# Rows of the split operands moved to the weights' place modulo 256 bytes

## The reference

```
y = swiglu(rmsnorm(h, g1), w_gu, w_down);  h = h + 0.5 * rmsnorm(y, g2)
proj = rmsnorm(h, g3) @ w_in               # q, k, v of three branches, and gates
branches: neighbourhood, sliding-window and differential attention
          (second stack: sliding-window, forgetting attention, a gated linear recurrence)
merged = sum over n of sigmoid(gate_n) * (branch_n @ w_branch[n])
h = h + rmsnorm(merged @ w_out, g4)
...
swiglu(x) = (silu(x @ w_gate) * (x @ w_up)) @ w_down      # inner width 2816
```

## The kernel before

| tile | before |
|---|---|
| `wh`, `wl` | 128 in every slot and every k |
| `uh`, `ul` row k | 192 + 64 k: 192, 0, 64, 128, 192, ... (rows 2112 bytes apart) |
| `obh`, `obl` row k | 32 + 64 k: 32, 96, 160, 224 |
| `mh`, `ml` row k | 160 + 64 k: 160, 224, 32, 96, ... |
| `gx`, `gb` | 96 (rows 2048 bytes apart) |
| `gu` | 128 (rows 2048 bytes apart) |
| `bh`, `bl` | 96 (rows 1024 bytes in use) |

## Time and profile before

### The profile page before, as it was taken

The page is one execution under the profiler, slowest core; times in us unless marked ns, Lnnn a source line. Parts: engine busy times, 40 slices in busy tenths (PEclk is TensorE's granted clock), DMA queues, the critical chain, the costliest instruction groups (busy, mean ns, idle before and its releaser), DMA issues. The chain is left out here.

```text
span 3400.5 us, 51734 instructions
## 1 busy us (share of the span) xinstructions
PE 3351.0 (99%) x20422; PEld 2960.8 (87%) x20422; DVE 2442.6 (72%) x3936; ACT 1690.7 (50%) x3071; POOL 849.2 (25%) x607
## 2 busy tenths in 40 slices
PE   9999999999999999999999999999999999999998
PEld 7999887888889998999887888899988888888998
DVE  7878765756697769777766666697768676649776
ACT  5545453635454445444554544454546374335543
POOL 3433111021063414432111021063400001206431
PEclk9999999999999999999999999999999999999999
DMA  4333433253223332333423263233333222322332
GB/s 137 106 100 113 115 90 86 67 147 93 82 91 104 108 100 78 103 106 112 117 75 93 70 152 96 69 99 102 105 96 96 86 80 69 106 88 93 98 108 81
DMA packets 118049, 332.79 MB, mean 98 GB/s; under 512 B 18984, under 2 KB 21800, under 8 KB 117808
## 3 DMA queue, kind: packets, MB, share of 16 engines
q1 hardware_dynamic: 105200, 306.30, 28.9%
q0 software_dynamic: 12320, 22.66, 3.2%
q10 hardware_dynamic: 288, 0.52, 0.1%
HBM read 306.23 MB, written 4.21 MB: 91 GB/s over the span
## 5 line engine op out<-in xcount | busy, mean ns | idle before, releaser
L1889 DVE TENSOR_TENSOR wl<-raw,wh 128x1024 fp32r<-128x1024 f32 (+2 forms) x633 | 800.7, 1269 | 277.4 <-ACT wh L1311 271.3
L1311 ACT ACTIVATE wh<-raw 128x1024 fp32r<-128x1024 f32 (+2 forms) x637 | 553.9, 875 | 393.8 <-PE PS L790 385.0
L790 PE MATMUL PS<-bh,wh 128*128 128x256 f32 x2520 | 711.1, 282 | 8.6 <-ACT tmp L1311 5.4
L790 PE MATMUL PS<-bh,wl 128*128 128x256 f32 x2520 | 708.0, 281 | 0.0
L790 PE MATMUL PS<-bl,wh 128*128 128x256 f32 x2520 | 707.9, 281 | 0.0
L790 PE MATMUL PS<-uh,wh 128*128 128x512 f32 (+2 forms) x1656 | 615.6, 372 | 12.0 <-DVE ul L1924 7.0
L790 PE MATMUL PS<-uh,wl 128*128 128x512 f32 (+2 forms) x1656 | 605.1, 365 | 0.0
L790 PE MATMUL PS<-ul,wh 128*128 128x512 f32 (+2 forms) x1656 | 603.6, 364 | 0.0
L790 PEld LDWEIGHTS PS<-bh,wh 128*128 128x128 f32 x2520 | 474.7, 188 | 14.8 <-DVE wl L1889 7.2
L790 PEld LDWEIGHTS PS<-bh,wl 128*128 128x128 f32 x2520 | 474.8, 188 | 0.7
L790 PEld LDWEIGHTS PS<-bl,wh 128*128 128x128 f32 x2520 | 474.8, 188 | 0.0
(11 more groups left out here) (268 smaller groups left out, 5766.3 us busy)
## 6 DMA issues: line engine op xcount, KB each, us to landing
raw<-in_gu SPq DMA_DIRECT2D x218, 512.0 KB, 3.2
raw<-in_win SPq DMA_DIRECT2D x139, 512.0 KB, 3.3
raw<-in_dn SPq DMA_DIRECT2D x80, 320.0 KB, 3.0
raw<-in_dn SPq DMA_DIRECT2D x40, 512.0 KB, 3.7
raw<-in_wbr SPq DMA_DIRECT2D x72, 256.0 KB, 2.7
raw<-in_wout SPq DMA_DIRECT2D x24, 512.0 KB, 3.2
raw<-in_dn SPq DMA_DIRECT2D x40, 256.0 KB, 2.7
raw<-in_wv SPq DMA_DIRECT2D x20, 512.0 KB, 3.2
```

Of the source, the lines that this page charges most:

```text
L790: return e.matmul(out, lhs, rhs, start=start, stop=stop, skip_group_check=True)
L1311: return e.activation(out, in_, f, scale=scale, **more)
L1889: tt(wl[:, c % 4, 0:n], src, wh[:, c % 4, 0:n], SUB).then_inc(*S.lo.up(("lo", c)))
```

## The change

Tiles get other addresses; nothing else is changed. `GAP` is 32 bytes, what takes X from its place (96) to the weights' (128). `uh`, `ul`, `mh`, `ml`, `obh` and `obl` become 512 columns wide, so that rows lie 2048 bytes apart and each begins at 128 modulo 256; `gx` (and behind it `b12`, `b21`) moves on by 32 bytes. v = 6 needs 528 columns and keeps the old rows under the names `uh6`, `ul6` (`y_u5` is what stage 5 leaves in their memory). `gu`, `gb`, `bh`, `bl` and the weights stay. `u_of` and `y_of` pick the tile and shift the columns by X0.

```
-        uh = sb("uh", [P, 8, TW], F32R, where["uh"])
-        ul = sb("ul", [P, 8, TW], F32R, where["ul"])
-        y_u = sb("y_u", [P, 8, TW], F32, where["uh"])
+        uh = sb("uh", [P, 8, 512], F32R, where["uh"])
+        ul = sb("ul", [P, 8, 512], F32R, where["ul"])
+        y_u = sb("y_u", [P, 8, 512], F32, where["uh"])
+        uh6 = sb("uh6", [P, 8, TW], F32R, where["uh"])
+        ul6 = sb("ul6", [P, 8, TW], F32R, where["ul"])
+        y_u5 = sb("y_u5", [P, 8, TW], F32, where["uh"])
...
+        GAP = (where["split"] - X) % 256
...
-        gx = sb("gx", [P, 6, 2, 512], F32R, X + 65536)
+        gx = sb("gx", [P, 6, 2, 512], F32R, X + 65536 + GAP)
...
-        mh = sb("mh", [P, 8, TW], F32R, X)
-        ml = sb("ml", [P, 8, TW], F32R, X + 8 * TW * 4)
+        mh = sb("mh", [P, 8, 512], F32R, X + GAP)
+        ml = sb("ml", [P, 8, 512], F32R, X + GAP + 8 * 2048)
...
-        obh = sb("obh", [P, 4, TW], F32R, XG + 10 * TW * 4)
-        obl = sb("obl", [P, 4, TW], F32R, XG + 14 * TW * 4)
+        XO = XG + 10 * TW * 4 + (GAP + 128) % 256
+        obh = sb("obh", [P, 4, 512], F32R, XO)
+        obl = sb("obl", [P, 4, 512], F32R, XO + 4 * 2048)
...
+        def u_of(v, part, k, c0, c1):
+
+            if v == 6:
+                return (uh6, ul6)[part][:, k, c0:c1]
+            return (uh, ul)[part][:, k, c0 - X0:c1 - X0]
...
+        def y_of(v, m, c0=X0, c1=TW):
+
+            return y_u5[:, m, c0:c1] if v == 5 else y_u[:, m, c0 - X0:c1 - X0]
...
-                            xh, xl = uh[:, kk, c0:c0 + cn], ul[:, kk, c0:c0 + cn]
+                            xh, xl = (u_of(v, i, kk, c0, c0 + cn) for i in range(2))
```

More of the change, by code:

```diff
@@ L816, in dense @@
                             E.wait_ge(S.dv, "m", v, kk)
-                            xh, xl = mh[:, kk, c0:c0 + cn], ml[:, kk, c0:c0 + cn]
+                            xh, xl = mh[:, kk, c0 - X0:c0 - X0 + cn], ml[:, kk, c0 - X0:c0 - X0 + cn]
                         else:
                             E.wait_ge(S.dv, "ob", v, job.tag[2], kk)
-                            xh, xl = obh[:, kk, c0:c0 + cn], obl[:, kk, c0:c0 + cn]
+                            xh, xl = obh[:, kk, c0 - X0:c0 - X0 + cn], obl[:, kk, c0 - X0:c0 - X0 + cn]
                         w1, w2 = wh[:, p % 4, P * k:P * k + P], wl[:, p % 4, P * k:P * k + P]
@@ L882, in first_two @@
                         w1, w2 = wh[:, p % 4, P * k:P * k + P], wl[:, p % 4, P * k:P * k + P]
-                        i = three(bank(job.banks[0]), w1, w2, uh[:, k, X0:TW], ul[:, k, X0:TW], k == 0, k == 7)
+                        i = three(bank(job.banks[0]), w1, w2, uh[:, k, :], ul[:, k, :], k == 0, k == 7)
                         if k == 7:
@@ L1054, in group_out @@
                         w1, w2 = wh[:, p % 4, P * k:P * k + P], wl[:, p % 4, P * k:P * k + P]
-                        i = three(bank(job.banks[0]), w1, w2, mh[:, k, X0:TW], ml[:, k, X0:TW], k == 0, k == 7)
+                        i = three(bank(job.banks[0]), w1, w2, mh[:, k, :], ml[:, k, :], k == 0, k == 7)
                         if k == 7:
@@ L1070, in values @@
                             w1, w2 = wh[:, p % 4, 512 * k2:512 * k2 + 512], wl[:, p % 4, 512 * k2:512 * k2 + 512]
-                            u1, u2 = uh[:, kk, tokens(j)], ul[:, kk, tokens(j)]
+                            u1, u2 = (u_of(v, i, kk, tokens(j).start, tokens(j).stop) for i in range(2))
                             mm(bank(vb[j]), u1, w1, kk == 0, False)
@@ L1377, in last @@
                         E.wait_ge(S.dv, "ev", job.tag, c)
-                        square("post", v, m, y_u[:, m, half(c)], 1.0, c)
+                        square("post", v, m, y_of(v, m, half(c).start, half(c).stop), 1.0, c)
                         return
@@ L1381, in last @@
                     square("post", v, m, o, 0.5, c)
-                    act(y_u[:, m, half(c)], o, ACT.Copy).then_inc(*S.aa.up(("y", v, m, c)))
+                    act(y_of(v, m, half(c).start, half(c).stop), o, ACT.Copy).then_inc(*S.aa.up(("y", v, m, c)))
                 ahead(p0)
@@ L1448, in part @@
                         E.wait_ge(S.mm, "job", job.tag, 0)
-                        act(y_u[:, m, X0:TW], bank(job.banks[0]), ACT.Copy).then_inc(*S.aa.up(("part", job.tag)))
+                        act(y_of(v, m), bank(job.banks[0]), ACT.Copy).then_inc(*S.aa.up(("part", job.tag)))
                 silu_plain(0)
@@ L1527, in out @@
                         square("post", v, m, bank(job.banks[0]), 0.5)
-                        act(y_u[:, m, X0:TW], bank(job.banks[0]), ACT.Copy).then_inc(
+                        act(y_of(v, m), bank(job.banks[0]), ACT.Copy).then_inc(
                             *S.aa.up(("y", v, m, 0)))
@@ L1668, in outputs @@
                         E.wait_ge(S.mm, "job", ("br", v, 0, 7), 0)
-                    act(obh[rows, t, X0:TW], bank(b)[rows, :], ACT.Copy).then_inc(*S.an.up(("oh", v, st, x)))
+                    act(obh[rows, t, :], bank(b)[rows, :], ACT.Copy).then_inc(*S.an.up(("oh", v, st, x)))
             def attention(v, st, fill):
@@ L1845, in mixer_2 @@
                     E.wait_ge(S.dv, "gelu", m, 3)
[L1846 removed]
+                    act(obh[:, m, :], lru[:, 4 + m, X0:TW], ACT.Copy).then_inc(*S.aa.up(("lru", m)))
                 tanh(v, 2, 0)
@@ L1994, in add_part @@
                 last = job.kind == "dn" and v == 7
-                y = h[:, m, c0:c0 + cn] if last else y_u[:, m, c0:c0 + cn]
+                y = h[:, m, c0:c0 + cn] if last else y_of(v, m, c0, c0 + cn)
                 i = tt(y, bank(job.banks[c], 0, cn), y, ADD)
@@ L2431, in rest @@
                     E.wait_ge(S.an, "oh", v, st, x)
-                    tt(obl[rows, t, X0:TW], bank(b)[rows], obh[rows, t, X0:TW], SUB).then_inc(
+                    tt(obl[rows, t, :], bank(b)[rows], obh[rows, t, :], SUB).then_inc(
                         *S.dv.up(("ol", v, st, x), *([("ob", v, BRANCH[st], t)] if x % 2 else [])))
@@ L2538, in low_c @@
                     E.wait_ge(S.an, "c_oh", v, x)
-                    tt(obl[:, x, X0:TW], GB[4 + x][:, X0:TW], obh[:, x, X0:TW], SUB).then_inc(*S.dv.up(("ob", v, 2, x)))
+                    tt(obl[:, x, :], GB[4 + x][:, X0:TW], obh[:, x, :], SUB).then_inc(*S.dv.up(("ob", v, 2, x)))
                 diagonal(0)
@@ L2729, in low_lru @@
                     E.wait_ge(S.aa, "lru", m)
-                    tt(obl[:, m, X0:TW], lru[:, 4 + m, X0:TW], obh[:, m, X0:TW], SUB).then_inc(*S.dv.up(("ob", v, 2, m)))
+                    tt(obl[:, m, :], lru[:, 4 + m, X0:TW], obh[:, m, :], SUB).then_inc(*S.dv.up(("ob", v, 2, m)))
                 ahead(reach(JOBS["g", v, 2, 0]))
```

38 lines of the change are left out of this document (20 added, 18 removed).

## The result

The changed kernel takes 3378.13 us (median of four runs, 3375.52 to 3382.65), against 3398.39 us for the kernel before, measured beside it (four runs, 3395.22 to 3400.6). The ratio is 0.9941, 95% interval 0.9927 to 0.9955: faster by 0.6%. The prediction was 3376 us in a range of 3366 to 3390. The profiled execution spans 3377.6 us, 22.9 less than the one before; the sum of the prediction was 22.8. By the medians the gain is 20.3 us, and the interval of the ratio allows 15 to 25, so the near agreement of 22.9 and 22.8 is more than the runs can vouch for.

What follows compares the result with a forecast made beforehand. TensorE was taken as the bound, busy 3351.0 of 3400.5 us. Terms 7.2 + 3.0 + 7.3 + 3.8 + 2.2 + 1.9 - 2.6 gave 22.8 us, hence 3377.7 profiled, 3376 us as median; range 3366 to 3390.

Steps and rivals of the forecast that it cites:

- The step: TensorE's 512-column matmuls: 226.7 ns each in a long run with all operands at one place modulo 256 bytes.
- gx, 7.2 us: FFN matmuls on gx: 1170 of 1650 gain 6.6 ns each, 7.7 us, less 0.5 us for entries.
- The 0.6 us of part 0: 96 gx matmuls opening each of five FFNs: saving waited for again behind them, counted as nothing; otherwise 3.2 us more.
- no free moment: VectorE during part 0 and behind it: full, 6.00 of 6 us in both stretches shown, so TensorE waits for its splits.
- uh in the mixers, 7.3 us: uh, ul in two mixers, 2 x 1032 matmuls: 4.2 us from fills between attention units, 3.1 from the others.
- the price of an entry: Start of each run at the weights' place: about six matmuls to reach the faster step, 20 ns lost.
- a fill of six: Six matmuls between attention units in the mixers: should take about as long as now.
- uh in the FFNs, obh, mh, values: Other 512-column matmuls: 744 on uh, 864 on obh, 432 on mh, 384 values; gains 3.0, 3.8, 2.2, 1.9 us.
- Halves, 2.6 us lost: 1548 matmuls of 256 columns on uh, gx and mh: 1.7 ns dearer each at the weights' place.
- The projections never settle: Rival: uh, obh, mh and values stay at 230 ns; gain 13.3 us, about 3385 us; chance 0.15.
- Slower: Rival: uh and ul mixed at one place settle on 240 ns, costing 36 us, 3430 us; chance 0.05.
- It does nothing: Rival: gu's step comes from something other than its place modulo 256 bytes; 3398.7 us, chance 0.08.

Runs made afterwards that it cites:

- e1: Loop of matmuls alone, computation left out, moving rows at eight places modulo 256: 48 matmuls of 512 columns take 10.88 us at the weights' place, 11.20 at 160.
- e4: The changed kernel with uh, ul, mh, ml, obh, obl 128 bytes further and gx back at 96: 3401.38 us, ratio 1.0006 to the kernel before.
- e2: The kernel before with gx alone moved by 32 bytes: 3393.4 us, ratio 0.9987.
- e3: The changed kernel with gx back at its old place (96): 3384.36 us, ratio 0.9959 to the kernel before.
- e8: Matmuls alone, stretches of 6 to 48 behind small ones, weights' place against place 96: shorter by 8.5 ns (6), 24 (12), 64 (18), 264 (48).
- e9: The changed kernel with the pairs' operands bh, bl (and gb) at the weights' place too: 3382.39 us, ratio 0.9947 to the kernel before.
- e10: Loop of 256-column matmuls alone at three places, six forms of distances, banks and neighbours: at place 64, 96 matmuls take 11.32 us in e1's form.
- e5: The changed kernel with rb and par moved behind X, so bh and bl lie 64 bytes below the weights: 3376.56 us, ratio 0.9928 to the kernel before.
- e7: e5 with VectorE multiplying only the first 128 of 512 columns of each pair's gated product: 3364.94 us, ratio 0.9895 to the kernel before.

## Why the prediction was right, point by point

**The step.** Right. `gx` at 227.1, values at 226.7, `obh` and `mh` in the two mixers at 230.9 and 226.9 ns with their entries, from 233 to 236 before. e1 and e4 show the cause as it was put: the place against the weights, modulo 256 bytes. Why the chip is faster there no run shows. The Trainium skill ("TensorE: Matmul & The Clock Gate", section "Step-by-step: what each phase is for") has two independent read ports, from which the prediction drew the rival that the place could not matter; the runs here do not agree with that: 226.7 against 233.3 ns for the same instructions.

**gx, 7.2 us.** Right in size and in its cover. The matmuls gained 10.25 us, the pairs gave 3.5 back (3.1 of it in the five gaps), 6.8 in sum. The 0.6 us of part 0 that were to be waited for again are waited for again, in all five FFNs, and e2 and e3 tie that to `gx`. That it is VectorE that they wait for, as the prediction says, is not settled: GpSimd's sums and ScalarE's copy of them come in at the very moment at which VectorE is free (975.53 and 975.52), and no run removed the work of either at this place. Nor has VectorE "no free moment": between the two stretches of the earlier trace rows it stands for 0.52 us until ScalarE's `wh` is there.

```profile
968.47 2.30 DVE L1889 TENSOR_TENSOR wl<-raw,wh 128x512 fp32r<-128x512 f32 x1 [0.52 <-ACT wh L1311]
```

**uh in the mixers, 7.3 us: mis-sized, 5.3 measured.** The step that failed is the price of an entry, "about six matmuls to fall into the faster step, and loses about 20 ns". It rested on one stretch of nine at one k, where the first six were compared with the last three. e8 shows some ten matmuls and 56 ns. In the kernel the 148 fills gained 2.6 us where 4.2 were predicted: 80 stretches of six 4 ns each (a fill of six "about as long as now", as predicted), 44 of twelve 18 ns each (26 without one that a dip of the clock met), 24 of eighteen 64 ns each. The other matmuls gained 2.6 instead of 3.1: the eight jobs of gates inside the two stretches of 312 (see the rivals, below) gained 4.9 ns a matmul, those in stretches of 12 to 48 less, from entries again.

**uh in the FFNs, obh, mh, values.** 3.6, 4.7, 2.5 and 1.9 against 3.0, 3.8, 2.2 and 1.9. `obh` and `mh` gained 5.4 and 5.8 ns a matmul, where the 5.0 of `uh` was taken. These errors and those of the halves and the mixers cancel; that the sum, 22.8 against 22.9, is closer than its terms is luck.

**Halves, 2.6 us lost: 1.2.** The sign was right and the size too large: `gx` paid 1.3 ns a matmul, `mh` 1.1, the moved `uh` 0.3 (its waits in the sum), where 1.7 was taken. e9 shows the like on the pairs: 1.6 ns on the steps under 150 ns (118.3 to 119.9), 1.1 on average with the waits, which became shorter.

**The rivals.** "The projections never settle" would have given 13.3 us at a step of 230 ns; plain jobs settle at 226.7 in every k (5.44 us for 24). "Slower" needed a mean step above 232.8 ns; the two mixers' long stretches of 312 went from 72.64 to 70.86 us. "It does nothing" is what e4 measured, for rows at another place.

## What to carry to other kernels

Where TensorE is the bound and runs long stretches of float32r matmuls of 512 columns, compare where the moving rows and the weights begin, modulo 256 bytes; a tile of the same kernel that is faster than its like is a sign to look there. A settled rate is worth only what remains of a stretch behind its entry: measure the entry in a stretch of the kernel's own length before pricing short ones. And what a loop measures alone (113.3 ns) is a bound, not a price, until the same step is seen inside the kernel, and seen in all of its steps: a median of 117 hid that some pairs ran at 113.3.

## What the runs showed of the hardware that was not expected

- At 64 bytes above the weights' place 512 columns take 228.9 ns, between 226.7 and 233.3; at 64 below they are as dear as elsewhere (233.3).
- For 256 columns the best place is not the weights' (120.0 ns) but 64 bytes below it, with two rhythms at the same addresses, 117.8 and 113.3 ns, in loops (e1, e10) and in the kernel (e5, e7).
- The way into the fast step lasts ten matmuls and is the same in eleven of every twelve entries of e8 with stretches of twelve and more; the twelfth is 32 ns shorter.
- VectorE's `wl<-ws,wh` on 1024 columns takes 1.21 us in the median of the 120 rows of the changed kernel with no GpSimd operation beside it, and 2.31 us in the median of the 50 rows with one.
